# The first two projection units share x's splits, and 512-column weight tiles move 32 bytes

## What is computed

```python
h = rms_norm(x, norm_mix[l])        # x * rsqrt(mean(x^2)) * gain
z = h @ w_in[l]                     # 2048 -> IN_WIDTH, 128 columns of z at a time in the kernel
z_a, z_b, z_cq, z_ckv_c, z_ckv_s, z_ckv_w, z_cg = jnp.split(z, split_at, axis=-1)
```

## Time and profile before

| what | value |
|---|---|
| median of three runs | 3297.06 us (3294.58 to 3297.74) |
| profiled execution, its own time | 3295.73 us |
| its span | 3293.9 us |
| granted TensorE clock, mean | 0.997 |
| TensorE busy with matmuls | 3266.9 us, 99% of the span |
| VectorE, ScalarE, GpSimd busy | 66%, 49%, 28% |

### The profile page before, as it was taken

One profiled execution on the slowest core, in us unless ns is written; L12 is line 12 of the kernel. 1 busy time (PEld: TensorE's weight loads), 2 busy tenths in 40 slices (PEclk: granted clock), 3 DMA queues, 4 the chain that ended last, 5 costly groups with the idle time before them and its releaser, 6 DMA issues.

```text
span 3293.9 us, 48400 instructions
## 1 busy us (share of the span) xinstructions
PE 3266.9 (99%) x19112; PEld 2859.3 (87%) x19112; DVE 2170.3 (66%) x3068; ACT 1621.6 (49%) x2692; POOL 912.7 (28%) x815
## 2 busy tenths in 40 slices
PE   8999999999999999999999999999999999999998
PEld 7989888888888897788888888889788888888887
DVE  6668677654676668778764477555778775457654
ACT  4557464444444545555443344444655544344443
POOL 2434132210232224254320033112336331013221
PEclk9999999999999999999999999999999999999999
DMA  7544546755566554555655556555355566555554
GB/s 258 189 166 148 175 158 210 234 192 188 190 189 194 186 187 134 159 169 184 191 189 195 185 189 190 193 190 179 123 175 170 187 191 194 190 187 190 188 195 143
DMA packets 188280, 604.57 MB, mean 184 GB/s; under 512 B 36597, under 2 KB 41573, under 8 KB 188054
## 3 DMA queue, kind: packets, MB, share of 16 engines
q1 hardware_dynamic: 188054, 601.47, 56.7%
HBM read 599.16 MB, written 8.00 MB: 184 GB/s over the span
## 4 chain that ended last, share of the span: by engine, by line
PE 91%; DVE 5%; ACT 3%; issue 1%; POOL 1%; DMA 0%; DVEq 0%; POOLq 0%; ACTq 0%; SPq 0%
PE ps L1825 90%; DVE wl L2433 2%; ACT sS L2267 1%; ACT wh L2171 1%; PE ps L1828 1%; DVE sS L2437 1%; POOL acc L2792 0%; DVE x L2441 0%; DVE xr L2433 0%; DVE den L2577 0%; ACT tA L2171 0%; DMA wt<-in_w_in 0%; DVE ua L2441 0%; POOL qc L2792 0%; ACT tG L2424 0%
## 5 line engine op out<-in xcount | busy, mean ns | idle before, releaser
L2433 DVE TENSOR_TENSOR wl<-wt,wh 128x1024 fp32r<-128x1024 f32 (+2 forms) x1104 | 1466.4, 1360 | 312.7 <-ACT wh L2171 296.4
L1825 PE MATMUL ps<-x,wh 128*128 128x512 f32 x4448 | 1563.4, 394 | 11.9 <-DVE x L2441 9.5
L1825 PE MATMUL ps<-x,wl 128*128 128x256 f32 x4448 | 1255.2, 282 | 0.0
L2171 ACT ACTIVATE wh<-wt 128x1024 fp32r<-128x1024 f32 (+2 forms) x1104 | 1117.4, 1051 | 275.2 <-PE ps L1825 236.2
L1825 PEld LDWEIGHTS ps<-x,wh 128*128 128x128 f32 x4448 | 837.0, 188 | 192.8 <-DVE wl L2433 13.9
L1825 PEld LDWEIGHTS ps<-x,wl 128*128 128x128 f32 x4448 | 842.6, 189 | 0.6
L1825 PE MATMUL ps<-ua,wh 128*128 128x512 f32 (+1 forms) x2432 | 832.0, 386 | 0.0
L1825 PE MATMUL ps<-ua,wl 128*128 128x256 f32 x2368 | 667.4, 282 | 0.0
L2433 DVE TENSOR_TENSOR tB<-ps,tA 128x256 f32<-128x256 f32 x422 | 177.1, 423 | 724.3 <-ACT tA L2171 724.2
L2171 ACT ACTIVATE tA<-ps 128x256 f32<-128x256 f32 x422 | 159.6, 382 | 945.0 <-PE ps L1825 944.8
L1825 PE MATMUL ps<-ub,wh 128*128 128x512 f32 x1536 | 536.6, 390 | 0.0
(11 more groups left out here) (233 smaller groups left out, 1855.7 us busy)
## 6 DMA issues: line engine op xcount, KB each, us to landing
wt<-in_w_up SPq DMA_DIRECT2D x384, 512.0 KB, 4.4
wt<-in_w_down SPq DMA_DIRECT2D x384, 512.0 KB, 4.8
wt<-in_w_in SPq DMA_DIRECT2D x156, 512.0 KB, 4.7
wt<-in_w_o SPq DMA_DIRECT2D x64, 512.0 KB, 4.5
wt<-in_w_out SPq DMA_DIRECT2D x32, 512.0 KB, 4.2
wt<-in_w_vb SPq DMA_DIRECT2D x16, 512.0 KB, 4.2
wt<-in_w_va SPq DMA_DIRECT2D x16, 384.0 KB, 3.7
wt<-in_w_vsl SPq DMA_DIRECT2D x8, 512.0 KB, 6.1
```

Of the source, the lines that this page charges most:

```text
L1825: return eng.matmul(o, l, r, start=start, stop=stop, skip_group_check=True)
L2171: return eng.activation(o, i, ACT.Copy, **kw)
L2433: return eng.tensor_tensor(o, a, b, op)
```

## The change

It has two parts. (1) `first_units` runs units 28 and 29 together: for the same x slices first the one unit's products, then the other's, in stretches of 8, 8, 4, 4, 4, 4 slices; the four weight halves are split in halves of 512 columns (`split_half`) between groups of x slices, loads are issued in another order, and 19 matmuls on the constant tile `ones` (`WARM`, 128 columns, plain float32) stand ahead of everything on TensorE. With it the squares, the norm's sums (`mix_begin`) and its spread (`mix_end`) come one unit later, and the constants `c1` are loaded behind unit 32's step. (2) `wh` and `wl` become 64 bytes longer each, and the splits of value units of 512 columns are written, and read by TensorE, 8 columns (32 bytes) further in. All other uses start at column 0 as before.

```diff
+SHIFT = 8
+
+def first_column(name):
+    return SHIFT if name[2:] in VALUES and VALUES[name[2:]].width == 512 else 0
...
+WARM = 19
...
-    feed_order(ORDER1, "w_in")
+    for half in range(2):
+        for t in ORDER1[:2]:
+            feed.append(("w_in", (t,), half, False, HALF))
+    feed_order(ORDER1[2:], "w_in")
...
+    def first_units(evs):
+        gs = next_bank(), next_bank()
+        state["u"] += 2
+        for q, k0, k1 in ((0, 0, 8), (1, 0, 8), (0, 8, 12), (1, 8, 12), (0, 12, 16), (1, 12, 16)):
+            h = 2 * (k0 // 8) + q
+            for k in range(k0, k1):
+                tiles[h].append((gs[q], src_x(k), k == 0, k == KT - 1, None, k == KT - 1))
+                matmuls(h, k % 8)
+            if k1 % 8 == 0:
+                done[gs[q]] = tick("t_used", h)
+                give(("wh", h), done[gs[q]])
+        pending.extend(zip(evs, gs))
...
-    for half in range(2):
-        prep_upto(half + 1)
-        for k in range(8 * half, 8 * half + 8):
-            step("xsplit", k)
...
-    prep_upto(4)
...
+    step("begin")
+    step("warm")
+    step("x_in", 0)
+    send_upto(1)
+    step("x_in", 1)
+    send_upto(3)
+    step("x_in", 2)
+    send_upto(4)
+    step("x_in", 3)
+    send_upto(5)
+    step("ident_in")
...
+    x_splits(0, 4)
+    split_half(0, 0)
+    split_half(0, 1)
+    x_splits(4, 8)
+    split_half(1, 0)
+    split_half(1, 1)
+    split_half(2, 0)
+    x_splits(8, 12)
+    split_half(3, 0)
+    x_splits(12, 14)
+    split_half(2, 1)
+    x_splits(14, KT)
+    split_half(3, 1)
...
-        after_unit.append(mix_end)
+            run_pending()
+        after_unit.append(lambda: at3.append(mix_end))
...
-        if t == 29:
+        if t == 30:
             at3.append(lambda: x_squares(8, KT))
-        if t == 30:
+        if t == 31:
             at13.append(mix_begin)
-        unit([(True, True, ev)], KT, X2, ahead=1 if t == 30 else 2)
+        if t == 32:
+            step("c1_in")
+
+        unit([(True, True, ev)], KT, X2, ahead=2)
...
-        wh = [sb(f"wh{i}", [P, HALF], F32R) for i in range(4)]
-        wl = [sb(f"wl{i}", [P, HALF], F32R) for i in range(4)]
+        wh = [sb(f"wh{i}", [P, HALF + 16], F32R) for i in range(4)]
+        wl = [sb(f"wl{i}", [P, HALF + 16], F32R) for i in range(4)]
...
+            def warm():
+                w.wait_ge(S.g_const, 1)
+                for _ in range(WARM):
+                    mm(bM[:, 0:P], ones[:, :], ones[:, :], True, True)
...
-                w.wait_ge(S.v_lo, at["v_lo", h])
+                w.wait_ge(S.v_lo, at["v_lo", h, 0] if h < 4 and k0 < 4 else at["v_lo", h])
...
+                    if h < 4 and k == 4:
+                        w.wait_ge(S.v_lo, at["v_lo", h])
...
-                o, c = ps[:, p.bank[g], 0:wide], slice(i * wide, (i + 1) * wide)
+                c0 = SHIFT if wide == 512 else 0
+                o, c = ps[:, p.bank[g], 0:wide], slice(c0 + i * wide, c0 + (i + 1) * wide)
```

More of the change, by code:

```diff
@@ L698, in residual, with x_splits @@
         return ev
[L701 to L708, removed]
-    for half in range(2):
-        prep_upto(half + 1)
-        for k in range(8 * half, 8 * half + 8):
+    def x_splits(k0, k1):
+        for k in range(k0, k1):
             step("xsplit", k)
@@ L714, in make_plan, with split_half @@
             tick("v_x2", "mix", k)
-    prep_upto(4)
+    def split_half(h, c):
+        step("split_half", h, c)
+        if c == 0:
+            take(("wh", h), "wh", h)
+            tick("a_hi", h, 0)
+            tick("v_lo", h, 0)
+            return
+        tick("a_hi", h)
+        give(("wt", h), tick("v_lo", h))
+    step("begin")
[9 more added lines that the diff above has]
+    step("ident_in")
+    for h in range(4):
+        where.append(("hl", h))
+        tiles.append([])
+    state["hl"] = state["prepped"] = 4
+    x_splits(0, 4)
[11 more added lines that the diff above has]
+    split_half(3, 1)
     def x_squares(k0, k1):
@@ L727, in x_squares @@
                 give(("S", j), ("g_acc", at["g_acc", "mix", KT - 2]), ("v_acc2", at["v_acc2", "mix", KT - 1]))
-    x_squares(0, 8)
     step("w2_in")
@@ L888, in nsa_head @@
         give("bO", ("v_u", at["v_u", "nsa", h]))
-    for t in ORDER1:
+    first_units([project("raw", (0, i)) for i in range(2)])
+    prep_upto(7)
+    x_squares(0, 8)
+    for t in ORDER1[2:]:
         if t in VALUES:
@@ L899, in make_plan @@
             continue
-        if t in (28, 29, 30, 31):
-            ev = project("raw", ((t - 28) // 2, (t - 28) % 2))
+        if t in (30, 31):
+            ev = project("raw", (1, t - 30))
         else:
             ev = project("ksl", t - 32 if t < 34 else t - 34)
-        if t == 29:
+        if t == 30:
             at3.append(lambda: x_squares(8, KT))
-        if t == 30:
+        if t == 31:
             at13.append(mix_begin)
-        unit([(True, True, ev)], KT, X2, ahead=1 if t == 30 else 2)
+        if t == 32:
+            step("c1_in")
+        unit([(True, True, ev)], KT, X2, ahead=2)
         if t == 31:
@@ L1746, in _ @@
                         eng.dma_start(memory(15), I["mem"][:, 15, :]).then_inc(d_mem[c], 16)
+                elif kind == "ident_in":
+                    eng.dma_start(idt[:, :], I["c2"][:, C_ID:C_ID + P]).then_inc(d_ident, 16)
                 elif kind == "c1_in":
-                    eng.dma_start(idt[:, :], I["c2"][:, C_ID:C_ID + P]).then_inc(d_ident, 16)
                     eng.dma_start(c1[:, :], I["c1"]).then_inc(d_c1, 16)
@@ L2113, in _ @@
             for kind, *key in p.steps:
-                if kind == "mm":
+                if kind == "warm":
+                    warm()
+                elif kind == "mm":
                     weights(*key)
@@ L2275, in _ @@
             for kind, *key in p.steps:
-                if kind == "split":
+                if kind == "warm":
+                    w.wait_ge(S.g_const, 2)
+                    copy(tS[:, 0, 0:4], mhalf[:, :])
+                elif kind == "split_half":
+                    h, c = key
+                    w.wait_ge(d_w[h], 16)
+                    cols = slice(HALF // 2 * c, HALF // 2 * (c + 1))
+                    copy(wh[h][:, cols], wt[h][:, cols]).then_inc(S.a_hi)
+                elif kind == "split":
                     h, i = key
@@ L2279, in _ @@
                     let_go(w, "wh", h)
-                    wide = feed[i][4]
-                    copy(wh[h % 4][:, 0:wide], wt[i % NWT][:, 0:wide]).then_inc(S.a_hi)
+                    c, wide = first_column(feed[i][0]), feed[i][4]
+                    copy(wh[h % 4][:, c:c + wide], wt[i % NWT][:, 0:wide]).then_inc(S.a_hi)
                 elif kind == "sum":
@@ L2613, in _ @@
             for kind, *key in p.steps:
-                if kind == "split":
+                if kind == "split_half":
+                    h, c = key
+                    w.wait_ge(S.a_hi, at["a_hi", h] if c else at["a_hi", h, 0])
+                    cols = slice(HALF // 2 * c, HALF // 2 * (c + 1))
+                    tt(wl[h][:, cols], wt[h][:, cols], wh[h][:, cols].bitcast(F32), ALU.subtract).then_inc(S.v_lo)
+                elif kind == "split":
                     h, i = key
                     w.wait_ge(S.a_hi, at["a_hi", h])
-                    wide = feed[i][4]
-                    tt(wl[h % 4][:, 0:wide], wt[i % NWT][:, 0:wide], wh[h % 4][:, 0:wide].bitcast(F32),
+                    c, wide = first_column(feed[i][0]), feed[i][4]
+                    cols = slice(c, c + wide)
+                    tt(wl[h % 4][:, cols], wt[i % NWT][:, 0:wide], wh[h % 4][:, cols].bitcast(F32),
                        ALU.subtract).then_inc(S.v_lo)
```

## The result

The changed kernel takes 3309.23 us (median of five runs, 3306.74 to 3311.11) against 3294.58 for the kernel before on the same chip: a ratio of 1.0041, 95% interval 1.0031 to 1.0052. It is 14.6 us slower where 4.6 us faster was forecast (3292.5, with a range of 3288.5 to 3297). The profiled execution has a span of 3304.6 us, 10.7 more than that of before.

A forecast was written before the change was run, and what follows sets the result against it. The prediction took TensorE's work plus its start and small gaps to bound the kernel. Net 2.7 us from the start plus 1.9 from the 32-byte shift gave 4.6, so 3297.06 - 4.6 = 3292.5 us, range 3288.5 to 3297.

The forecast's parts named there:

- The start: First two units run together: third unit starts at 19.6 instead of 22.91, 3.3 us earlier; net 2.7, bounds 0.5 and 3.8.
- The term for the constant products: 19 warm-up matmuls on TensorE raise the clock before real pairs; if it stays low, two units end 1.6 us later, at 21.2.
- the 0.6 given back: Later squares, norm sums and spread, possible `xc` wait and moved `c1` load: -0.6 us counted against the start's gain.
- The shift: Value matmuls of 512 columns, moved 32 bytes, lose 0.005 us each: 384 x 0.005 = 1.9 us gained; upper bound 7.7.
- The reason given: 512-column value matmuls pay 0.005 us more than the moving x because their operand starts 32 bytes off modulo 64.
- The step that failed: Part 2: the three engines do the same operations with other addresses; no cost entered for the pairs.
- the sum: Whole kernel: 2.7 from the start plus 1.9 from the 32 bytes, 4.6 us gained, 3292.5.
- The moved buffers: Rival: `wh` and `wl` 1 and 3, 64 bytes off modulo 128, lengthen pairs; at 3 ns 9.5 us net loss, 3306.5; chance 0.05.

The follow-up runs named there:

- experiment 1: New start alone, without the longer buffers and the shift, against the kernel before: 3291.77 us against 3295.12, ratio 0.9989 (0.9981 to 0.9998).
- experiments 7: New start without longer buffers and shift, tile `gap` left out, so moving operands start at 32 modulo 128 like the weights: 3320.56 us, one run.
- 8: New start without longer buffers and shift, `gap` left out, 32-byte tile ahead of `wh`, both operands at 64 modulo 128: 3307.99 us against 3295.19, ratio 1.0044.
- 11: Changed kernel with small tiles between buffers, each `wh` and `wl` at 160 modulo 256, `gap` left out: 3291.25 us against 3295.35 before, ratio 0.9988.
- 6: New start without longer buffers and shift, 64-byte tile ahead of `wh`, so stationary and moving operands both go 64 bytes on: 3290.05 us, one run.
- 3: Changed kernel with `SHIFT = 0`, so start and longer buffers but no shift: 3307.9 us against 3295.12 for the kernel before, ratio 1.0040.
- 9: New start without longer buffers and shift, `gap` of 64 bytes, distance 64 of moving from stationary operand: 3335.61 us, one run.
- 5: New start without longer buffers and shift, `gap` 64 bytes longer, so only the moving operand goes 64 bytes on: 3316.64 us, one run.
- 10: New start without longer buffers and shift, `gap` of 160 bytes, distance 160 of moving from stationary operand: 3292.52 us, one run.
- experiment 4: Changed kernel with 64-byte tiles behind each `wh` and `wl`, all again at 32 modulo 128: 3297.7 us against 3295.12 before, ratio 1.0008.

## Why the prediction was wrong

- **The start** was forecast with its third unit at 19.6 and measured at 20.13; net gain 2.7 forecast, 3.3 by the medians of experiment 1 (its interval goes from 0.7 to 6.3). Right, in mechanism and nearly in size. The term for the constant products (1.6 us if they fail) measured 2.0. The gain at the third unit was 0.5 smaller than forecast (2.8, not 3.3), and the 0.6 given back was not seen: the lead is still 2.8 us at 420 us. That the net comes so near 2.7 is luck: two errors cancel.
- **The shift** was forecast as 384 x 0.005 = 1.9 us. It gave 0.7 in the changed kernel, since the 64-byte step put only buffer 0 (229.1 ns) where it had to be; 230.6, 232.5 and 233.6 in the others. With all buffers in place it gave 4.5 ns, as sized. The reason given, a start off a multiple of 64 bytes, was wrong.
- **The step that failed** is the one in front of the sum: "ScalarE, VectorE and TensorE do the same operations with other addresses", priced at nothing for all pairs. The moved buffers were a rival with a chance of 0.05, as "a weight read there makes a pair longer", at a price per pair of 1 to 3 ns; measured were 4.8 and 3.9 ns in the two buffers named, 2.2 in the mean over all pairs, 18 us where the sum had nothing. The place and the buffers were right, the chance far too low, and the mechanism was another: not the stationary operand's place but the distance of the moving one from it.

What the runs showed of the distance (start of the moving operand less start of the stationary one, modulo 256 bytes; mean from one start to the next):

| distance | pair (512 and 256 columns), ns | value matmul, 512 columns, ns |
|---|---|---|
| 0 | 346.7 or 353 by turns; in the mean 351.0, 349.2 (experiments 7, 8) | 228.6 (11), 228.4 (7 and 8), 229.1 (changed kernel, buffer 0) |
| 32 | 346.8 (before, 1, 6, 11), 346.5 (changed kernel, buffer 0) | 233.1 (3, buffer 1) |
| 64 | 353.0 (9) | 230.6 (changed kernel, buffer 1) |
| 96 | 350.1 (5), 350.7 (changed kernel, buffer 3) | 233.3 (10) |
| 128 | not seen | 232.5 (changed kernel, buffer 2) |
| 160 | 346.7 (10, and 4 within a half), 347.2 (changed kernel, buffer 2) | 233.8 (5) |
| 192 | not seen | 233.6 (changed kernel, buffer 3), 233.4 (9) |
| 224 | 351.5 (changed kernel, buffer 1) | 233.1 (before, 1) |

The rows of the changed kernel include the first pairs of a half, which pay by themselves (experiment 4). Pairs want 32 modulo 128, values 0 modulo 256. That the distance is what decides is shown for pairs by experiments 5 and 6 together, at two distances; the rest of the table is one layout each, and at distance 0 it does not decide alone. What in the chip makes it so was not tried, nor whether it is the two operands of one matmul that meet or those of neighbouring ones: in a pair the next weights are loaded under the running matmul, and both fit.

The Trainium skill, "SBUF — State Buffer", Specifications, has lines of 16 bytes; all places tried are multiples of 32, so that rule would have left the times alike. The traces don't agree with it as a full account: 346.7 to 353.0 ns a pair.

## What to carry to other kernels

A buffer made longer moves every buffer behind it, and in a kernel that one engine binds by thousands of equal instructions that is an edit to each of them: price 1 ns times their number before pricing it at nothing. When TensorE is the bound, note the start-to-start time of its commonest matmul before and after any change of the memory layout, and keep the distance between the moving and the stationary operand as it was, modulo 256 bytes here. A gain of 3 us at the start is better told from the trace's own marks than from totals, whose interval goes from 0.7 to 6.3 us here (experiment 1).

## What was not expected of the hardware

- Pairs of matmuls on the same data took 346.7 to 353.0 ns by the two operands' places, 1.8% of a pair and 1.4% of the kernel's time from best to worst (3290.05 us in experiment 6, 3335.61 with distance 64, one run each).
- At distance 0 the same pairs at the same addresses ran at 346.7 ns in one part of an execution and at 353 in another (experiments 7 and 8).
- A change of place from one weight half to the next, 128 bytes modulo 256, costs the first pairs of the half: 6 and 5 ns for the first two in buffers 0 and 2, 3 ns for the first and nearly nothing for the second in 1 and 3 (experiment 4).
- How soon the clock rose varied: the 38 constant records took 6.0 us in the changed kernel and 7.0 in the new start alone, from the same first start at 1.67 us. They go from 0.21 us apart to 0.11, and in the new start alone they do so ten records later.
- The profiled execution of experiment 11 had one wait of 2.6 us for POOL's power behind a longer addition (4.7 us in three waits for it, 1.0 in the changed kernel); its own time, 3293.88, is the highest of that kernel's eleven.
